# A decoder trunk's mixers on one Trainium2 core: the four turn tables written in another order

## The reference

```python
for i in range(DEPTH):
    h = rmsnorm(x, W['norm_mix'][i])
    cp = h @ W['w_in'][i]
    ya, sh, Sa = rwkv7_mixer(cp[..., :COLS_A], ...)                  # group A, 6 heads of 64
    yb, Sb = retention_mixer(cp[..., COLS_A:COLS_A + COLS_B], ...)   # group B, 4 heads
    yc, cv, hc = mamba2_mixer(cp[..., COLS_A + COLS_B:], ...)        # group C, 6 heads
    x = x + jnp.concatenate([ya, yb, yc], axis=-1) @ W['w_out'][i]
    h = rmsnorm(x, W['norm_ffn'][i])
    x = x + (swiglu(h, ...) if i % 2 == 0 else moe_swiglu(h, ...))   # top 2 of 8 experts
y = rmsnorm(x, W['norm_final'])
```

## Time and profile before

| | |
|---|---|
| three executions | 1313.04 us median, 1309.83 to 1313.10 |
| profiled execution | 1312.32 us, its span 1310.4 us |
| mean granted TensorE clock | 0.952 of full |
| busy: TensorE (PE) / DVE / ACT / POOL | 1235.7 / 914.3 / 716.2 / 132.6 us |
| matmuls | 12189 |
| read from HBM | 225.36 MB |
| mixer of layer 0, of layer 1 | about 22 to 285, about 550 to 818 us |

### The profile page before, as it was taken

The page is one execution under the profiler, slowest core; times in us unless marked ns, Lnnn a source line. Parts: engine busy times, 40 slices in busy tenths (PEclk is TensorE's granted clock), DMA queues, the critical chain, the costliest instruction groups (busy, mean ns, idle before and its releaser), DMA issues.

```text
span 1310.4 us, 30345 instructions
## 1 busy us (share of the span) xinstructions
PE 1235.7 (94%) x12189; PEld 1101.7 (84%) x12189; DVE 914.3 (70%) x1489; ACT 716.2 (55%) x1109; POOL 132.6 (10%) x161
## 2 busy tenths in 40 slices
PE   7987999899999999998899998999999999999996
PEld 7977888799999999997787987887888788788785
DVE  7574655657555556857266565679989998998996
ACT  6633345434432434473144444478778778777874
POOL 1121210120000000102113002000110100101010
PEclk9988899879999999999679987999999999999998
DMA  7321331065445444242024105459879988897993
GB/s 292 114 84 33 114 112 35 18 225 192 148 154 163 146 153 137 71 134 74 29 77 164 34 14 195 162 182 363 324 255 342 337 315 295 332 345 260 356 326 115
DMA packets 63848, 236.52 MB, mean 180 GB/s; under 512 B 7536, under 2 KB 7760, under 8 KB 63088
## 3 DMA queue, kind: packets, MB, share of 16 engines
q1 hardware_dynamic: 60960, 221.46, 48.6%
q0 software_dynamic: 2336, 12.81, 2.5%
q10 hardware_dynamic: 432, 0.52, 0.1%
HBM read 225.36 MB, written 8.09 MB: 178 GB/s over the span
## 4 chain that ended last, share of the span: by engine, by line
PE 79%; DVE 11%; issue 5%; ACT 4%; DMA 1%; DVEq 0%; ACTq 0%
PE bank L632 12%; PE bank L634 11%; PE bank L633 11%; PE bank L1446 8%; PE bank L1423 6%; PE bank L1425 6%; PE bank L1424 6%; PE bank L626 3%; DVE wlo L2018 2%; ACT whi L1509 2%; PE bank L1343 2%; PE bank L821 1%; PE bank L1388 1%; PE bank L1372 1%; DMA out_o_ret<-srt 1%
## 5 line engine op out<-in xcount | busy, mean ns | idle before, releaser
L1509 ACT ACTIVATE whi<-wraw 128x1024 fp32r<-128x1024 f32 x407 | 428.8, 1059 | 373.3 <-PE bank L634 311.8
L2018 DVE TENSOR_TENSOR wlo<-wraw,whi 128x1024 fp32r<-128x1024 f32 x407 | 502.1, 1247 | 175.9 <-ACT whi L1509 165.1
L632 PE MATMUL bank<-hh,whi 128*128 128x320 f32 x576 | 195.0, 339 | 13.1 <-DVE Dx L2132 6.3
L633 PE MATMUL bank<-hl,whi 128*128 128x320 f32 x576 | 185.7, 322 | 0.0
L634 PE MATMUL bank<-hh,wlo 128*128 128x320 f32 x576 | 185.5, 322 | 0.2 <-issue 0.2
L1423 PE MATMUL bank<-whi,hh 128*128 128x512 f32 (+1 forms) x384 | 147.6, 384 | 3.2 <-DVE wlo L2018 2.8
L1425 PE MATMUL bank<-wlo,hh 128*128 128x512 f32 (+1 forms) x384 | 143.4, 373 | 0.0
L1424 PE MATMUL bank<-whi,hl 128*128 128x512 f32 (+1 forms) x384 | 143.3, 373 | 0.0
L632 PEld LDWEIGHTS bank<-hh,whi 128*128 128x128 f32 x576 | 115.0, 200 | 25.1 <-issue 9.7
L632 PE MATMUL bank<-rawh,whi 128*128 128x320 f32 x384 | 120.1, 313 | 0.5 <-DVE rawl L2589 0.3
L634 PE MATMUL bank<-rawh,wlo 128*128 128x320 f32 x384 | 119.3, 311 | 0.0
(11 more groups left out here) (439 smaller groups left out, 2068.9 us busy)
## 6 DMA issues: line engine op xcount, KB each, us to landing
wraw<-in_w SPq DMA_DIRECT2D x410, 512.0 KB, 5.0
smb<-in_s_ssm POOLq DMA_DIRECT2D x2, 1536.0 KB, 7.9
out_o_ssm<-smb POOLq DMA_DIRECT2D x2, 1536.0 KB, 6.8
cst<-in_consts SPq DMA_DIRECT2D x1, 2049.0 KB, 13.1
srw<-in_s_rwkv POOLq DMA_DIRECT2D x2, 768.0 KB, 5.4
out_o_rwkv<-srw POOLq DMA_DIRECT2D x2, 768.0 KB, 3.6
x<-in_x SPq DMA_DIRECT2D x2, 640.0 KB, 4.8
cBs<-cB SPq DMA_DIRECT2D x16, 80.0 KB
```

The lines of the kernel that those rows point to most:

```text
L632: mm(out, hi, rh, start=first, stop=False)
L633: mm(out, hi, rl, start=False, stop=False)
L1509: af(whi[:, ring % HI, :], wraw[:, POS[ring], :], ACT.Copy).then_inc(S("slot_hi"), 1)
L2018: tt(wlo[:, POS[ring], :], wraw[:, POS[ring], :], whi[:, ring % HI, :].bitcast(F32), ALU.subtract).then_inc(S("slot_split"), 1)
```

## The change

The four tables hold the same turns in another order; every turn issues the same instructions with the same waits, and the turns of one part keep their order among themselves. Two lines of PE's table, and POOL's whole:

```diff
 PE_TURNS = """
-    in in in in in in in in prep in in in in in in in prep in in in prep in in in in in inv2 inv1 inv0 in inv1 inv2
-    inv0 in inv2 in prep inv2 inv0 inv1 in in inv1 inv0 inv2 prep inv1 in inv0 inv2 in inv1 inv0 cb2 cb2 sS sS sS
...
+    in in in in in in in in prep in in in in in in in prep in in in prep in in in in inv0 inv2 in inv1 in in inv1
+    inv2 in inv2 inv0 inv2 inv1 in inv0 in prep inv1 inv0 inv2 prep in inv1 sS inv0 inv0 in inv2 inv1 cb2 cb2 sS
...
 POOL_TURNS = """
-    prep prep shift conv conv prep conv conv conv conv xv conv conv rot xv xv xv xv mb0 rot mb1 mb2 rt1 conv mb1 rt2
-    mb2 mb2 rt2
+    prep prep conv conv conv conv rot prep conv xv xv xv conv xv rot conv mb0 mb1 shift conv xv mb2 rt2 rt1 mb2 conv
+    rt2 mb2 mb1
```

More of the change, by code:

```diff
@@ L183 @@
+    in in inv1 rw2 nS cb0 cb0 nS rw2 in rw2 in inv1 nS rw2 in in mb0 cb0 in in mb0 tok0 tok0 rw2 in in rt0 mb0 in
+    tok0 in mb0 in rt0 mb0 in rw0 mb1 in rw0 in mb1 rw0 rw0 rw0 mb1 rt0 rw0 mb1 rt0 rw0 rw0 cb1 rw0 cb1 cb1 mb1 tok1
+    rw0 tok1 mb2 tok1 rw0 mb2 rw1 rt0 mb2 rt0 rw1 rw1 rt1 mb2 rw1 mb2 rt1 rt1 rt1 rw1 rw1 rt1 rw1 rw1 rt1 rw1 rt2
+    rw1 rt2 rw1 out rt2 out rt2 out rt2 rt2
 """
 ACT_TURNS = """
-    dt in in in in prep prep in in in in prep prep in in prep in in prep in in prep prep in in in in in in in in
@@ L186 @@
[L186 to L189, removed]
+    in in in dt in prep in in prep in prep in in in prep prep in in prep in in in prep prep in in in in in in in in
@@ L190 @@
+    in in in in in prep prep in in conv conv in sS in tok2 dt tok2 dt conv in in in prep conv tok2 conv in in dt
+    conv in rw2 in in conv in in in rw2 in in in mb0 mb0 rw2 in in mb0 in in tok0 in mb0 tok0 mb0 tok0 in mb1 rt0
+    rw0 mb1 in mb1 mb0 rw2 rw0 mb1 rw0 rw0 mb1 rt0 tok1 rw0 tok1 mb2 tok1 rt0 mb1 mb2 mb2 rt0 rw0 rw1 mb2 mb2 rt1
+    out rt1 rt0 rt1 rw1 rt1 mb2 out rw1 rw1 rt1 rw1 rt2 rw1 rt2 rt2 rt2 rt2
 """
 DVE_TURNS = """
-    prep in in in in in in in prep in in in in in in prep in in in prep in prep prep in prep prep in inv2 inv1 in
@@ L193 @@
[L193 to L197, removed]
@@ L198 @@
-    mb0 rw2 mb1 rw0 mb1 mb1 mb1 mb1 mb1 mb1 rw0 cb1 cb1 cb1 mb1 mb1 rw0 mb1 mb2 rw0 rt0 rw0 rw0 rt0 rw0 rw1 mb2 rt0
-    rt0 mb2 mb2 rt0 rw1 rt1 rt1 mb2 mb2 mb2 rw1 rt1 rt1 mb2 mb2 rt1 rt1 rw1 mb2 rt1 out out rt2 rt2 rw1 rw1 rw1 rw1
-    rw1 rt2 rt2 rt2 rt2 rt2 rt2
+    prep in in in in in in in prep in in in in in in in prep in in prep prep prep in in prep prep in inv2 prep in in
+    inv0 inv2 inv1 inv1 in inv0 inv0 inv1 inv2 inv2 in inv1 inv2 conv inv0 conv inv1 conv conv in inv0 inv2 inv2
+    conv inv1 conv inv0 conv inv1 conv inv0 inv2 in inv1 conv inv0 cb2 conv conv inv0 in inv0 conv conv inv0 inv1
@@ new lines @@
+    cb2 conv dt conv inv0 dt inv1 dt dt dt dt dt dt inv0 dt inv1 dt conv dt conv conv in in conv dt conv conv inv0
+    conv conv in conv conv conv dt inv1 conv in conv rw2 xs inv1 in xs nS xs nS rw2 nS nS rot nS cb0 inv1 nS rot in
+    in rot cb0 cb0 mb0 rw2 in mb0 rt0 mb0 rw2 rw2 rt0 in mb0 rw2 mb0 mb0 mb0 mb0 mb0 mb0 in rw0 mb1 mb1 rw0 rw0 mb1
+    mb1 mb1 rw2 mb1 mb1 rt0 rw0 mb0 cb1 mb1 cb1 cb1 mb1 mb1 rw0 mb2 rw0 rw0 rw0 mb1 rt0 rw1 rw0 mb2 mb2 rt0 mb2 rw1
+    rt1 rt1 rt0 mb2 mb2 mb2 rt1 rw1 mb2 mb2 rt1 out rt1 rw1 rt1 rt2 rt2 rw1 rt0 mb2 rw1 rw1 rw1 rt1 rt2 rw1 rt2 rt2
```

7 lines of the change are left out of this document (2 added, 5 removed).

## The result

The changed kernel takes 1300.26 us in the median of four executions (1299.45 to 1303.99), beside 1311.43 for the kernel before: a ratio of 0.9923, 95% interval 0.9894 to 0.9952. Forecast were 1306 and 1296 to 1318; the narrower band of 1301 to 1310, to which the prediction gave 0.48, it misses by 0.7. By the medians the change is worth 11.2 us. The profiled execution, 1303.99 us with a span of 1302.0, is the longest of the four; it stands 8.3 us under the profiled one of before, where the sum of the prediction had 7.1.

A forecast was written before the change was run, and what follows sets the result against it. PE, busy 94% of the span, was taken as the bound, losing time in the mixers to late neighbours, instruction supply and granted clock. Six terms sum to -7.1 us: 1305.2 for the profiled run, 1306 for the median, range 1296 to 1318.

The forecast's parts named there:

- Term 1: Start of the inverses: long idle gap cut to 1.8 us, half-clock stretches behind the waits go; -5.5 us, both layers.
- Term 2: Inverse stretch (87 to 136, 614 to 676 us): supply stalls stay, fewer dense halves at half clock; -1 and -2 us.
- Term 3: The nS place, with rot.1 moved ahead: PE's 1.7 us wait for Wm goes, a 1.5 hand-over comes; -0.4 us.
- Term 4: Between in.48 and in.49: four turns of small sets cover 1.2 of 1.4 us a layer waiting for ACT; -2.4 us.
- Term 5: Newly adjacent sets: inv0.6 waits for DVE's Wm, tok2.2 for an ACT copy; +3.2 us for both layers.
- Term 6: Mixer's tail: DVE's out.2 ahead of rt2's last turns, rw1.5 and rw1.6 adjacent; +1.0 us for both layers.
- A: Inverse stretches: instruction supply sets the pace, the start's gain is lost at the next starved block; 1312.7 us, chance 0.22.
- B: Start, both layers: half clock spreads, five dense halves in each layer lose 1.5 us; 1320 us, chance 0.14.
- C: Inverse steps: POOL's port block finds no cover and hits DVE, 2.8 us a layer; 1311 us, chance 0.06.
- D: Starts lose idle and half clock (-5.4 each), half the inverse stretch's bound comes back; 1297 us, chance 0.10.

The follow-up runs named there:

- s_start: New order only in the start (to 76 us), old order behind, against the kernel before: 1317.35 us, ratio 1.0049.
- s_start_inv: New order for start and inverse stretch (to 140 us), old order for the rest, against the kernel before: 1303.88 us, ratio 0.9947.
- s_inv: New order only in the inverse stretch (76 to 143 us), old order elsewhere, against the kernel before: 1302.20 us, ratio 0.9928.
- e_shift: Kernel before with 32 more small products (128 PE instructions) repeated ahead of inv2.1 in layer 0 alone: 1314.95 us, ratio 1.0046.
- s_tail: Old order to 209 us, new order from there to the mixer's end, against the kernel before: 1301.82 us, ratio 0.9936.
- e_dense2: Kernel before with 48 useless dense matmuls, 12 behind inv1.4 and 12 behind inv0.6 in both layers: 1309.02 us, ratio 0.9991.
- s_inv_tail: New order in inverse stretch and tail, old order in start and middle, against the kernel before: 1291.40 us, ratio 0.9843.
- e_gap: Kernel before with 18 useless dense matmuls in PE's idle gap of 3.08 us, in both layers: 1308.18 us, ratio 0.9988.

## Why the prediction was right, and where not

The direction and the time within the range were right, and the size was near: 8.3 us in the profiled pair and 11.2 by the medians, for 7.1 in the sum. That the sum came so near is luck. The terms were wrong by far more than the sum, and cancelled: in the profiled pair the start cost 2.2 us for a forecast gain of 5.5, and the stretch of the inverses gave 12.1 where terms 2 and 5 together had nothing. By the prediction's own signs its account is refuted: it was to be wrong if the issue waits shrank by over 3 us, and they shrank by 5.4; it asked for one of 3.9 among them, and the longest is 2.5; and the cZ wait, which was to go, grew.

- **Term 1, the start, -5.5.** Failed: +2.2 in the profiled pair. The step "The long gap is cut to 1.8" took the landing of the moved shift to be 66.7 us. It landed at 70.25. The step took DVE's times ahead of it as unchanged, but in the new order DVE reaches L2172 at 65.35 instead of 61.71, behind as many shifts and low parts: ACT's s_rn comes 6 us later, and the shift at 62.47 waits 1.63 us for ACT's sh_out. So the new order waits 1.20 and 2.17 us for two shifts, with 0.5 and 0.8 earlier on, where before had one wait of 3.08. Alone the new start costs 0.5%, with the new stretch behind it about 0.2%. The clock part (half-clock stretches gone) came true in the changed kernel's profile but not in those of s_start and s_start_inv. Filling the old gap showed the mechanism that the term rested on to be real. What was wrong is the belief that the change removes that gap.
- **Term 2, the inverse stretch, -3.** Right in sign, and the term most undersized: the stretch gave 12.1 us in the profiled pair and 0.72% alone in s_inv, of which 0.35% or 4.6 us are the order of the sets without POOL's. The step "so I let the supply stalls stand" failed: in the stretches around the inverses they come to 10.2 us for 15.6 (4.0 and 6.2 for 6.9 and 8.7), 5.4 less. The clock gave 6.8 us of busy time there, 1.3 of it by the stretch at 81.3 that term 1 counts, for 3 in the term. The two go together: of the half-clock stretches of before, those at 112.1, 624.1 and 641.1 begin during a supply stall of 2.2 to 3.9 us or within 0.5 us of its end. The count of 384 that it read was right, and the block has its like in 256 instructions, matmuls and loads. Where an edge falls decides which stall is long (e_shift), how closely the sets stand decides their sum (s_inv and its like).
- **Term 3, nS and rot.1, -0.4.** The mechanism was right and the size right for the sum: L850's 1.7 us is gone, L626 waits 1.22 and 0.38. The middle as a whole still cost 2.2 us in the profiled pair. The move of rot.1 was undersold: it is worth 5 to 6 us where nothing takes its gain away, and rw2.2 with nS.1 directly behind takes some of it. The cover for POOL's work on its new place held: the Trainium skill's rule ("SBUF — State Buffer", section "SBUF: two separate sides") of one engine blocking the other is borne out by 4.00 us against 1.22 for the same instruction with and without rot.1 beside it, and by 4.08 with it put back.
- **Term 4, cZ, -2.4.** Failed: the wait grew to 1.91. The step that failed was to count four turns of small sets as cover for ACT; one of them, rw2.6, needs ACT itself, and its function table, so it pushes cZ back by a load of 1.28.
- **Term 5, new neighbours, +3.2.** Right: 2.5 (L828 for Wm) and 0.9 (L976 for tok).
- **Term 6, the tail, +1.0.** Missed: the new tail alone gives 0.64%, some 8 us, of which 1.5 lie outside the half clock. "+1.0 for both layers" counted waits alone, and even these it had the wrong way: L945 and L918 gave 6.5 back, against 4.9 of new ones. No term stood for the clock of the tail, where most of what s_tail gains lies. In the changed kernel's own profile the tail gave 0.7 us and has as much half clock as before, so the profiled 8.3 us owe nothing to it.
- **Rivals.** A (the supply takes back what is won) is out: s_inv keeps its gain and e_dense2 adds work at no cost. B's mechanism, a clock that falls behind the start's new waits, happened in s_start, with 3.4 us twice in layer 0 and once in layer 1; that is no more than before had. C did not occur. D's time of 1297 came nearer than its chance of 0.10 would have it, and s_inv_tail went beyond it. One leg of D held, the clock of term 2's stretch; the other did not, since the starts gave nothing.

Of the Trainium skill's rule on the clock ("TensorE: Matmul & The Clock Gate", section Part 1: idle gaps let it fall) e_gap is the direct proof here. The stretch of 13.7 us at 641.1, which the prediction took as evidence against the rule, is none: PE had waited 2.73 us until 640.85. Yet there are stretches with no wait ahead of them. In before, PE goes through 96 small products without a pause and the clock falls behind them:

```profile
774.54 2.97 PE L626 MATMUL bank<-cde,smb 128*64 128x8 f32 x96
...
777.70:781.10 3.40, 3.40 (x38) 2.62 (x38) 3.37 (x9) 0.85 (x2) 0.00 (x0) 0.50 0.00 0
```

In the changed kernel the stretches at 120.9, 237.0 and 766.0 begin so too, with no more than 0.1 us of idle time in the three us ahead. What brings the clock down there is open.

## What to carry to other kernels

When a table reorders everything, build mixtures by stage before believing an explanation of the sum: here a start that costs, a stretch and a tail that gain made up one small number, and leaving out the new start and middle gave twice the gain (1291.4 us, 1.6% under before). Read the busy time of the bound engine beside its idle time; if the gain is in the busy time of the same matmuls, it is the clock, and gaps and long runs of small products are what to look for. One profile shows where the gain of one execution lies; the new tail here gave 6 us in four of the eight places where it was profiled and next to nothing in the others. Before moving a turn on PE forward to cover a wait for an engine, check that the moved turn does not itself call on that engine.
